# A hybrid network on one core: norm factors of the queries moved into the softmax, and eight weight blocks in the seven-product form

## The reference, cut to what matters

```
proj = rms_norm(x) @ w_in                     # q, k, v, iq, ik, iw, a, c, g
q = partial_rope(rms_norm(q, q_norm_g))       # 8 heads of 128; 32 of 128 are rotated
k = partial_rope(rms_norm(k, k_norm_g))       # 2 heads of 128
score = sum_h relu(iq_h . ik) * iw_h          # picks 64 keys of each query
p = softmax(where(valid, q . k * 128**-0.5, -inf));  y_attn = (p . v) @ w_attn_out
y_conf = silu(layer_norm(conv31(a_val * sigmoid(a_gate)) + b)) @ w_conf_out
c_b, c_c, c_x = split(c, 3)
y_sc = (c_b * conv3(c_c * c_x)) @ w_sc_out
x = x + (g0*y_conf + g1*y_attn + g2*y_sc) @ w_o;  x = x + ffn(rms_norm(x))
```

## Time and profile before

| | |
|---|---|
| median of 3 runs | 1989.9 us (1989.87 to 1993.44) |
| the profiled execution | 1987.63 us, its span 1985.8 us |
| PE busy | 1969.3 us, 99% |
| VectorE, GpSimd, ScalarE busy | 1161.3 us (58%), 1074.8 us (54%), 395.6 us (20%) |
| granted clock of TensorE | full (1.00) over the span |
| weights and other reads from HBM | 294.35 MB |

### The profile page before, as it was taken

One profiled execution on the slowest core, in us unless ns is written; L12 is line 12 of the kernel. 1 busy time (PEld: TensorE's weight loads), 2 busy tenths in 40 slices (PEclk: granted clock), 3 DMA queues, 4 the chain that ended last, 5 costly groups with the idle time before them and its releaser, 6 DMA issues. The chain is left out here.

```text
span 1985.8 us, 36677 instructions
## 1 busy us (share of the span) xinstructions
PE 1969.3 (99%) x14578; PEld 1848.7 (93%) x14578; DVE 1161.3 (58%) x2950; ACT 395.6 (20%) x972; POOL 1074.8 (54%) x717
## 2 busy tenths in 40 slices
PE   9999999999999999999999999999999999999999
PEld 7788889998899999999999889999999999999998
DVE  4244435887976567524887887467713367454441
ACT  2241521111321222110111222122102015120000
POOL 1000048682165588758673145578776674348883
PEclk9999999999999999999999999999999999999999
DMA  5314445444344445444444343454454442445444
GB/s 210 132 43 143 152 151 170 137 170 134 128 149 149 149 170 170 164 155 170 158 153 152 128 149 123 154 173 170 166 173 151 146 149 86 142 153 173 170 160 138
DMA packets 42984, 298.67 MB, mean 150 GB/s; under 512 B 4928, under 2 KB 6080, under 8 KB 8832
## 3 DMA queue, kind: packets, MB, share of 16 engines
q1 hardware_dynamic: 42560, 295.42, 43.4%
q10 hardware_dynamic: 256, 0.92, 0.3%
HBM read 294.35 MB, written 1.05 MB: 149 GB/s over the span
## 5 line engine op out<-in xcount | busy, mean ns | idle before, releaser
L712 PE MATMUL bank<-arena,ring 128*128 128x128 f32 (+2 forms) x3814 | 606.7, 313 | 1.7 <-DMA ring<-wstream 0.8
L712 PEld LDWEIGHTS bank<-arena,ring 128*128 128x128 f32 x3814 | 543.0, 191 | 45.8 <-ACT arena L1284 3.1
L712 PE MATMUL bank<-xn,ring 128*128 128x128 f32 (+3 forms) x3232 | 508.1, 313 | 4.1 <-DVE arena L2328 4.1
L712 PEld LDWEIGHTS bank<-xn,ring 128*128 128x128 f32 (+1 forms) x3232 | 458.0, 191 | 41.6 <-issue 9.2
L712 PE MATMUL bank<-arena 128*128 128x128 f32 (+5 forms) x2856 | 369.0, 285 | 0.0
L712 PEld LDWEIGHTS bank<-arena 128*128 128x128 f32 (+1 forms) x2856 | 342.9, 192 | 10.1 <-issue 2.8
L712 PE MATMUL bank<-arena,h_res 128*128 128x128 f32 x2600 | 310.8, 276 | 1.9 <-POOL h_res L1711 1.2
L712 PEld LDWEIGHTS bank<-arena,h_res 128*128 128x128 f32 x2600 | 299.4, 192 | 4.8 <-POOL h_res L1711 2.4
L1707 POOL TENSOR_TENSOR arena<-ring 128x1024 f32<-128x1024 f32 (+1 forms) x96 | 229.5, 2391 | 131.0 <-DMA ring<-wstream 130.8
L1707 POOL TENSOR_TENSOR h_res<-ring 128x1024 f32<-128x1024 f32 (+1 forms) x91 | 212.4, 2335 | 108.5 <-DMA ring<-wstream 93.2
L1751 DVE SCALAR_TENSOR_TENSOR bank<-arena,par,bank 128x256 f32<-128x256 f32 x640 | 259.5, 483 | 14.9 <-issue 7.5
(11 more groups left out here) (230 smaller groups left out, 1791.5 us busy)
## 6 DMA issues: line engine op xcount, KB each, us to landing
ring<-wstream SPq DMA_DIRECT2D x264, 1024.0 KB, 4.8
ring<-wstream SPq DMA_DIRECT2D x16, 768.0 KB, 4.2
cst<-consts SPq DMA_DIRECT2D x1, 2488.0 KB, 14.6
h_res<-tokens SPq DMA_DIRECT2D x2, 544.0 KB, 5.3
out<-arena SPq DMA_DIRECT2D x4, 256.0 KB, 5.3
arena<-arena ACTq DMA_DIRECT2D x4, 160.0 KB, 4.3
ring<-wstream SPq DMA_DIRECT2D x2, 288.0 KB, 2.8
par<-params SPq DMA_DIRECT2D x1, 541.5 KB, 9.1
```

The lines of the kernel that those rows point to most:

```text
L712: return pe.matmul(o, lhs, rhs, start=start, stop=stop, skip_group_check=True)
```

## The change

Three parts go together.

1. **Norm factors of the queries.** They are no longer spread over the partitions and multiplied into q. `row_sums` gives the queries' sums with the tokens on the partitions (16 matmuls with one moving column in a layer, 8 with two in C) beside those of the keys; ACT takes the root and DVE the reciprocal of a 128x16 tile, which DVE then multiplies by plus and minus the softmax's scale (`q_scale`). Its columns are the scale of the softmax's exponential, one value for a token, and the factor of the maximum: the instruction at L2037, a `tensor_scalar`, becomes a `tensor_tensor` over 128x1. The q gain goes into q by four ACT copies of 128x512 in a layer (`gained`); in C, the product of both gains goes into k. Of the spread, one pair stays in a layer (k) and two in C. The copies of 16 rows for the rotation are two of q, issued early, and two of k; the rotation of 32 rows is split likewise.
2. **cx0 in the seven-product form**: 4 blocks in a layer, 8 in all, with POOL's mixes, ACT's copies and DVE's unites for them.
3. **The order** around cx0. PE: one block of cx0, the spread of k, two blocks, index products, the last block; the sums of the layer norm one block of cx1 earlier. DVE: the unites of cx0 among the last taps, the rotation of iq behind the second of them, `ranked`'s first half ahead of the layer norm. POOL: in L0 the eight multiplications and two of the four additions now stand ahead of cx0's mixes, the other two behind.

```diff
-        pl(n + "cx0", "w_in_2", l, 2, 2, 8, two(co + 1024, co + 2048))
+        fast(n + "cx0", "w_in_2", l, 2, 2, lambda it, q: co + 1024 + 1024 * q + 256 * it)
...
-            def row_sums(key, n, weights, per, kind="side"):
+            def row_sums(key, queries, keys, weights, per, kind="side"):
...
-                for j in range(n):
-                    window = CONST[weights][0] + 16 - per * j
-                    ins = mm(b, slice(0, 16), slice(0, S), cst[:, window:window + 16], sq[:, j, 0:S],
-                             j == 0, j == n - 1)
+                a = CONST[weights][0] + 16
+                for t in range(2):
+                    for j in range(queries):
+                        col = S + 8 * t + per * j
+                        mm(b, slice(0, P), slice(col, col + per), sq[:, j, P * t:P * t + P], cst[:, a:a + per])
+                for j in range(keys):
+                    ins = mm(b, slice(0, 16), slice(0, S), cst[:, a - per * j:a - per * j + 16], sq[:, queries + j, 0:S],
+                             j == 0, j == keys - 1)
...
-                halves(L + "cx0", 0, 8, [P, P], x256, S)
-                spread(range(3))
-                halves(L + "cx0", 1, 8, [P, P], x256, S)
-                spread(range(3, 5))
-                halves(L + "cx0", 2, 8, [P, P], x256, S)
+                cx0(F, 0)
+                spread()
+                cx0(F, 1)
+                cx0(F, 2)
...
-                    act.activation(p_, p_, ACT.Exp, scale=scale, bias=small[:, k:k + 1],
+                    act.activation(p_, p_, ACT.Exp, scale=q_scale[:, 8 * t + h:8 * t + h + 1], bias=small[:, k:k + 1],
...
+                def gained(it):
+
+                    pair = slice(2 * it, 2 * it + 2)
+                    act.wait_ge(*e.at((L + "qk", "sq", 2 * it + 1)))
+                    act.activation(qk0[:, pair, :], qk0[:, pair, :], ACT.Copy,
+                                   scale=G(f"q_norm_g_2.{l}", 0)).then_inc(*e.step((L + "qg", it)))
...
-                        dve.tensor_scalar(small[:, k:k + 1], small[:, 16 + k:17 + k], -scale, None, ALU.mult).then_inc(*e.step((L + "sm", h, t)))
+                        dve.tensor_tensor(small[:, k:k + 1], small[:, 16 + k:17 + k], q_scale[:, 16 + 8 * t + h:17 + 8 * t + h],
+                                          ALU.mult).then_inc(*e.step((L + "sm", h, t)))
...
+            def rows_inverse(key, scale):
+                dve.wait_ge(*e.at((key, "q_rms")))
+                dve.reciprocal(q_scale[:, 0:16], q_scale[:, 0:16]).then_inc(*e.step((key, "q_inv")))
+                dve.wait_ge(*e.at((key, "q_inv")))
+                dve.tensor_scalar(q_scale[:, 16:32], q_scale[:, 0:16], -scale, None, ALU.mult).then_inc(*e.step((key, "q_minus")))
+                dve.wait_ge(*e.at((key, "q_minus")))
+                dve.tensor_scalar(q_scale[:, 0:16], q_scale[:, 0:16], scale, None, ALU.mult).then_inc(*e.step((key, "q_plus")))
...
+                convolved(200, 208)
+                cx0_in(0)
+                spread_norm(L + "qk", range(1), G(g("k_norm_g_2"), 0), qk0[:, 8:10, :], qk0[:, 8:10, :], L + "qkn")
+                convolved(208, 224)
+                cx0_in(1)
+                dve.wait_ge(iq_halves, 64 * (l + 1))
+                rotate_in_place(iq0[:, :, :], iq[:, :, :], "idx", slice(0, P), (L + "iqr",))
+                convolved(224, 232)
+                cx0_in(2)
                 dve.wait_ge(*e.at((L + "iws",)))
                 scores(0, 3)
-                convolved(218, 228)
+                convolved(232, 8 * CK)
+                cx0_in(3)
                 scores(3, 6)
-                convolved(228, 8 * CK)
                 scores(6, 8)
...
                 short_conv(0)
+                ranked(0, TOPK // 16)
...
                 branch_b(1)
-                ranked(0, TOPK // 16)
+                ranked(TOPK // 16, TOPK // 8)
                 branch_b(2)
-                ranked(TOPK // 16, TOPK // 8)
```

More of the change, by code:

```diff
@@ L157, in down_quarters @@
     return quarters(w, 256 * it, [2 * k for k in DOWN_PAIRS[q]], 1)
-FAST = [f"L{l}.{part}" for l in range(2) for part in ("a", "q", "k", "v", "iq", "g", "conf", "sc", "attn", "o", "up", "down")]
+FAST = [f"L{l}.{part}" for l in range(2) for part in ("a", "q", "k", "v", "iq", "g", "cx0", "conf", "sc", "attn", "o", "up", "down")]
 FAST += [f"C.{part}" for part in ("mqk", "mv", "rqk", "rv", "rg", "gate", "ret", "o", "up", "down")]
@@ L1459, in _ @@
                 b = e.bank_of((L + "qk", "sum"))
+                act.activation(q_scale[:, 0:16], psum[b][:, S:S + 16], ACT.Sqrt, scale=1.0 / P,
+                               bias=small[:, 62:63]).then_inc(*e.step((L + "qk", "q_rms")))
                 act.activation(tmp[0:16, 0, 0:S], psum[b][0:16, 0:S], ACT.Sqrt, scale=1.0 / P,
@@ L1568, in _ @@
             b = e.bank_of(("C.mqk", "sum"))
+            act.activation(q_scale[:, 0:16], psum[b][:, S:S + 16], ACT.Sqrt, scale=1.0 / 64,
+                           bias=small[:, 62:63]).then_inc(*e.step(("C.mqk", "q_rms")))
             act.activation(tmp[0:16, 0, 0:S], psum[b][0:16, 0:S], ACT.Sqrt, scale=1.0 / 64,
@@ L1738, in _ @@
                             pool.wait_ge(*e.at(event))
-                    if b == (L, "g", 11, 0):
+                    if b == (L, "cx0", 1, 1):
+                        for j in (6, 7):
+                            one = ac[:, 0, :] if j == 1 else sel[:, 0, :]
+                            event = (L + ".ln", "total") if j == 7 else (L + ".ln", "part", j)
+                            pool.wait_ge(*e.at((L + ".ac", j)))
+                            pool.tensor_tensor(out=sel[:, 0, :], in0=one, in1=ac[:, j, :], op=ALU.add).then_inc(*e.step(event))
+                            pool.wait_ge(*e.at(event))
                         gather(L + ".ln", S, sq)
@@ L2018, in _, with heads @@
                 ALU.add).then_inc(*e.frees(("L0.n1", "sum"), ("L0.n1", "mean")))
-            def heads(L, pr, scale, mask, between=None, beside=None):
+            def heads(L, pr, mask, between=None, beside=None):
                 def masked(h):
@@ L2291, in scores, with cx0_in @@
                             dve.wait_ge(*e.last())
+                def cx0_in(n):
+                    tiles = slice(n // 2 * 2, n // 2 * 2 + 2)
+                    out, cols = (scp[:, tiles, :], 2) if n % 2 else (ys[:, tiles, :], 0)
+                    unite((F, "cx0", n // 2, n % 2), out, cols)
+                for it in range(12):
+                    unite((F, "g", it, 0), sg[:, 2 * it:2 * it + 2, :], 0)
+                    if it < 11:
+                        convolved(90 + 10 * it, 100 + 10 * it)
+                convolved(200, 208)
[7 more added lines that the diff above has]
+                cx0_in(2)
                 dve.wait_ge(*e.at((L + "iws",)))
                 scores(0, 3)
-                convolved(218, 228)
+                convolved(232, 8 * CK)
+                cx0_in(3)
                 scores(3, 6)
-                convolved(228, 8 * CK)
                 scores(6, 8)
@@ L2532, in _ @@
             unite(("C", "rg", 1, 0), rg[:, 2:4, :], 0)
-            spread_norm("C.mqk", range(4), lambda p: "q_norm_w_3" if p < 2 else "k_norm_w_3", mqk0, mqk, "C.mqkn")
+            dve.tensor_tensor(q_scale[:, 32:33], G("q_norm_w_3", 0), G("k_norm_w_3", 0), ALU.mult).then_inc(*e.step(("C.gains",)))
+            dve.wait_ge(*e.at(("C.gains",)))
+            spread_norm("C.mqk", range(2), q_scale[:, 32:33], mqk0[:, 4:8, :], mqk[:, 4:8, :], "C.mqkn")
             for it in (2, 3):
```

103 lines of the change are left out of this document (50 added, 53 removed).

## The result

The changed kernel took 1994.8 us (median of 13 runs, 1992.31 to 1996.92), the kernel before 1989.9 (13 runs). The ratio is 1.0024, with a 95% interval from 1.0017 to 1.0032: 0.2% slower, where 8 us less were forecast and 1991 was the top of the range. A second series, beside other runs of before, gave 1994.53 and 1.0021 (1.0012 to 1.0030). The profiled execution took 1995.45 us, 7.8 more than the one of before.

The account below looks back on a forecast made before the run. TensorE, busy 1969.3 of 1985.8 us, was taken as the bound. Work 14.9 less and waits 6.9 more gave -8.0; 1987.6 - 8.0 + 2.3 = 1982 us, range 1973 to 1991.

Parts of the forecast that it names:

- the waits of the rotation: At the index products, TensorE waits 2.7 to 3.9 us for VectorE's iq rotation, delayed by GpSimd; 3.5 a layer, 7.0.
- of cb: At the layers' first cb blocks, TensorE waits 1.4 us each for VectorE, 2.8 against 4.1 before.
- of the heads: In heads 5 to 7, the maximum's factor held up by GpSimd makes TensorE 0.43 us late; 1.0 a layer, 2.0.
- of the first mix: In L0's first cx0 block, TensorE waits 1.0 us for GpSimd's mix, behind a multiplication and additions.
- the end of the wait at the layers' head 0: At the layers' first heads, 1.8 us of waits for `normalised` goes because `ranked` moved ahead of cb.
- Rival A: Rotation and maximum are not held up beside GpSimd; 6.6 us less than forecast, 1975 us, chance 0.17.
- B: GpSimd's second instruction also cuts in at the heads; waits 10.4 instead of 2.0, 1990 us; 0.15 together with D.
- C: Each head's loss at the 128x1 multiplication is met anew, 26.2 us in both layers; 2006 us, chance 0.08.
- rival D: A one-column record costs what a 256-column one does, 17.3 us instead of 7.9; 1991 us; 0.15 together with B.
- I take 7.9: New queries' sums on TensorE: 80 records at 0.098 us cost 7.9, range 3.9 to 9.0; net saving 1.1.
- My sign of being wrong: TensorE's busy time falling under 13 us, or waits for `normalised` above 5 us, would mean B or C.
- the 2.3 that I added: Added to the profiled execution's 1987.6 us to reach the median, as that execution was 2.3 below it.

Follow-up runs that it names:

- Version 5: Changed kernel with one-column matmuls apart, plus sixteen unused 128-column matmuls per layer filling TensorE's wait for the rotation: 1978.8 us, ratio 0.9948.
- version 4: Against the changed kernel, VectorE rotates iq ahead of the 16 taps and cx0's second unite; eight taps follow that unite: 1990.6 us, ratio 1.0003.
- version 1: Against the changed kernel, the layers' sixteen matmuls for the queries' sums have 128 moving columns instead of one: 1984.43 us, ratio 0.9974.
- version 2: Against the changed kernel, two one-column matmuls follow each 256-column matmul of the ik block instead of standing in a row: 1983.06 us, ratio 0.9971.
- version 7: Against version 2, cx0 back in the plain form, without its mixes, copies and unites, GpSimd's additions together again: 1976.65 us, ratio 0.9934.
- Version 8: Changed kernel with one-column matmuls apart, scalar maximum factor, earlier iq rotation, taps spread, `ranked` and layer-norm sums at their old places: 1975.08 us, ratio 0.9931.
- version 9: Against version 8, cx0 back in the plain form of before: 1980.1 us, ratio 0.9953.
- version 3: Against the kernel before, sixteen unused one-column matmuls added in each layer ahead of the ten sums of squares: 1998.51 us, ratio 1.0047.

## Why the prediction was wrong

**What held.** The costs of the wide matmul records (0.216, 0.112), the waits of the rotation (7.6 against 7.0), of cb (2.9 against 2.8), of the heads (1.8 against 2.0) and of the first mix (0.7 against 1.0), the end of the wait at the layers' head 0, and the mechanism of two of them: VectorE and GpSimd take turns when both read two tensors from SBUF. (Rotation: not one instruction of 2.5 among three, as I wrote, but all three are drawn out to 2.1 to 2.4.) Rival A is refuted by the rotation's 2.1 to 2.4 us for each instruction, rivals B and C by waits of only 1.8 us at the heads, rival D by 0.093 to 0.111 us for a one-column record. The expected sum of work and waits, -8.0, was right within a microsecond or so: without the 15.1 us of clock TensorE's busy time would be 14.1 less than before (forecast 14.9, which takes 1.0 for the net of the sums where its own step says 1.1), and what is not busy rose from 16.5 to 23.4, by 6.9 (forecast 6.9). Version 5, which keeps the rotation's delay but loses no clock, has a span of 1977.0 against 1985.8, 8.8 less.

**What failed.** The step "I take 7.9: the rows with 16 and with 128 columns differ so little that the load of the stationary operand must set both". It priced the new sums by the duration of a record at full clock, from six records that stood among wider ones. As the duration of a record this was nearly right: in a row at full clock it is 0.111 with one column (version 4) and 0.114 with 128 (version 1, 378.28 - 374.62 for 32), so 80 records take 8.9 in place of 7.9, about the 0.8 by which the work was off. The clock behind them was put at nothing, without a reason. Sixteen such matmuls in a row are another thing: TensorE was busy by its records, yet the granted clock fell to 0.50 within 4 us and everything behind them ran at half speed until 387.8. That is 5.0 us in each layer, 10 together (version 1 gives 10 back, version 2 by the ratios 10.5). The range for this term, from 3.9 to 9.0, could not contain it, since it looked only at the matmuls themselves.

The second step is "TensorE waits 2.7 to 3.9 [...] I take 3.5 a layer, 7.0". The wait was right, its price was not: behind a wait of 3.7 to 3.9 the clock is at 0.50 for 5 us, 2.5 us more in each layer, 5 together (in version 2's profiled execution the two falls cost 6.0; filling the wait, version 5, got 4.3 to 4.6 back). The trace of the kernel before had nothing that showed it, as its longest waits of 2.04 leave the clock at 1.00 and the group behind them at 14.05. I read the full clock in the earlier trace rows as a property of the kernel, not as something that the change could take away. The four possibilities that I laid out were about who waits for whom; none was about the clock, and its 15.1 us is even more than the distance between the forecast 1982 and the measured 1994.8, 12.8. My sign of being wrong, busy time falling by less than 13 us, came true (it rose by 1.0), but it did not point at B or C as I had said.

Most of what is left over, 2.3, is the 2.3 that I added to get from the profiled execution to the median. It is no constant: the changed kernel's profiled execution, 1995.45, is 0.65 above its median. The runs of the kernel before that stand beside the versions show what is in it. Of 53 executions on three chips, the 9 with a granted clock of 1.000 took 1988.2 us (median), the 24 with 0.999 took 1989.8, and the 20 with 0.998 took 1990.9. So the clock falls in some executions of the kernel before too, and the profiled one, with 1987.63, was of the first kind; where it falls no trace shows.

**Part 2 against part 1.** With the sums apart, the seven-product form of cx0 cost 6.4 us in the order of the change (versions 2 and 7) and gained 4.4 in a better order (versions 8 and 9). Of that 4.4, 1.7 is in the profiled executions a fall of the clock that only the plain form had. In the order of the change its saving of matmuls was outweighed: the two unites and the mix that it put ahead of and beside the rotation made a wait and a fall of the clock worth more.

## What to carry to other kernels

Where TensorE is the bound, price a change by what it does to the granted clock too: here a row of 32 records with one moving column each, and each wait of 3.2 to 4.1 us, was followed by microseconds at half clock that its own duration does not show. Put such a row's matmuls between wide ones, or give them columns that nobody needs. When an engine with a full queue makes TensorE wait, moving one item forward only moves the wait on, so look for what it meets next before counting on the gain. Version 8 spread the queue, and the wait that moved on was 2.4 in place of 3.4; it changed several things at once, and which of them did it was not separated.

## What the runs showed of the hardware that I had not expected

- Matmuls of 128 stationary columns with one moving column, 32 records in a row, brought the granted clock from 1.00 to 0.50 while TensorE's records had no gap; the same 32 with 128 moving columns, or two matmuls at a time between matmuls of 256, left it at 1.00. So did 16 records with two columns, 1.85 us.
- Behind the fall it stayed at 0.50 for about 10 us in the changed kernel, 6 to 7 in L0 of versions 3 and 4 and less in L1 of version 3 (a loss of 1.7 us), with TensorE busy throughout. So the same instructions do not always cost the same.
- In the profiled executions, waits of 3.2 to 4.1 us were each followed by a stretch at half clock, which cost from 1.7 (versions 1 and 4) to 3.2 us (version 2); waits of 1.5 to 2.0 were not; of the waits of 2.4 in versions 8 and 9 one of four was.
- Two VectorE multiplications over 128x1 took 2.39 us beside a GpSimd instruction of 2.37, and 0.28 without one beside them.
